# Mixed attention in a four-layer model: a mask moved from TensorE to VectorE, and a projection stage laid out anew

## The reference

```python
# first model, layers 0 and 3: three groups of 16 heads of 64; windows 128, 512, 2048, dilations 1, 4, 16
s = einsum("bnqhd,bnkhd->bnhqk", qb, kk) * scale
s = where(valid, s, NEG_INF)                 # window, dilation and causal mask
p = exp(s - logsumexp(s)); o = p @ vv        # groups are then weighed by their logsumexp
# second model
qa, ka, va, qb, ckv, iq, ik, iw = split(rmsnorm(h) @ w_in)
o_a = diff_attention(qa, ka, va)             # 4 heads: softmax 1 minus lambda times softmax 2
c = rmsnorm(ckv); q_lat = rmsnorm(einsum("blhd,hdc->blhc", qb, w_uk))
score = einsum("bqh,bqhk->bqk", iw, relu(iq . ik))   # 8 index heads
sel = top_k(score, 64)                       # keys that each query may see
o_b = softmax over sel of (q_lat . c + bias), times c, times w_uv
h = h + concat(o_a, o_b) @ w_out
```

## Time and profile before

| | |
|---|---|
| time, median of 3 runs | 2188.54 us (2186.72 to 2189.94) |
| profiled execution: its time, its span | 2189.12 us, 2187.3 us |
| TensorE busy in it | 98% of the span |
| VectorE busy, ScalarE busy | 68%, 46% |
| chain that ended last | 91% TensorE, 4% VectorE, 3% ScalarE |
| mean granted TensorE clock | 0.993 of full speed |

### The profile page before, as it was taken

How to read it: one execution, slowest core, us unless ns; L and a number is a source line. 1 busy time by engine, 2 the same in 40 slices (tenths; PEclk the granted TensorE clock), 3 DMA queues, 4 the chain that set the end, 5 groups by cost and what they waited for, 6 DMA issues and landing times.

```text
span 2187.3 us, 43087 instructions
## 1 busy us (share of the span) xinstructions
PE 2142.3 (98%) x16131; PEld 1962.9 (90%) x16131; DVE 1497.1 (68%) x2462; ACT 1005.9 (46%) x1348; POOL 483.7 (22%) x518
## 2 busy tenths in 40 slices
PE   7999999999999999999999999999999999999999
PEld 7998779988999988799889987799889998779998
DVE  6884778856688667588678847788565545566653
ACT  4334555544355553455443345555453334354342
POOL 2320004520124305034212200045213300201320
PEclk8999999999999999999999999999999999999999
DMA  5555225564645554245655552155545555305554
GB/s 177 192 179 186 77 84 182 183 204 168 206 151 191 194 181 145 68 154 191 207 165 177 191 180 90 68 179 186 203 155 172 168 178 182 104 13 162 184 185 142
DMA packets 299904, 350.28 MB, mean 160 GB/s; under 512 B 7588, under 2 KB 254950, under 8 KB 299814
## 3 DMA queue, kind: packets, MB, share of 16 engines
q1 hardware_dynamic: 298070, 347.05, 48.6%
q10 hardware_dynamic: 1360, 1.77, 0.2%
q0 software_dynamic: 384, 0.24, 0.0%
HBM read 346.35 MB, written 2.68 MB: 160 GB/s over the span
## 4 chain that ended last, share of the span: by engine, by line
PE 91%; DVE 4%; ACT 3%; DMA 2%; issue 1%; ACTq 0%; SPq 0%; DVEq 0%
PE ps L2260 26%; PE ps L2262 26%; PE ps L2261 26%; PE ps L2661 2%; PE ps L2632 1%; PE ps L2608 1%; PE ps L2619 1%; ACT w_hi L1200 1%; DVE w_lo L1634 1%; PE ps L2376 1%; PE ps L2371 1%; PE ps L2372 1%; PE ps L2308 1%; PE ps L2602 1%; DMA raw<-in_w_in_dram 0%
## 5 line engine op out<-in xcount | busy, mean ns | idle before, releaser
L1634 DVE TENSOR_TENSOR w_lo<-raw,w_hi 128x2048 fp32r<-128x2048 f32 (+3 forms) x311 | 697.1, 2241 | 456.9 <-ACT w_hi L1200 456.6
L2260 PE MATMUL ps<-a_hi,w_hi 128*128 128x256 f32 (+1 forms) x3176 | 899.4, 283 | 5.1 <-DVE w_lo L1634 4.7
L2262 PE MATMUL ps<-a_hi,w_lo 128*128 128x256 f32 (+1 forms) x3176 | 897.2, 282 | 0.0
L2261 PE MATMUL ps<-a_lo,w_hi 128*128 128x256 f32 (+1 forms) x3176 | 897.0, 282 | 0.0
L1200 ACT CAST w_hi<-raw 128x2048 fp32r<-128x2048 f32 (+3 forms) x319 | 589.9, 1849 | 557.0 <-PE ps L2262 531.7
L2260 PEld LDWEIGHTS ps<-a_hi,w_hi 128*128 128x128 f32 x3176 | 601.1, 189 | 11.5 <-DVE w_lo L1634 5.5
L2262 PEld LDWEIGHTS ps<-a_hi,w_lo 128*128 128x128 f32 x3176 | 602.0, 190 | 0.0
L2261 PEld LDWEIGHTS ps<-a_lo,w_hi 128*128 128x128 f32 x3176 | 598.8, 189 | 0.1
L2164 POOL TENSOR_TENSOR hs<-sg,cv 128x256 f32<-128x256 f32 x88 | 65.4, 743 | 672.3 <-DVE cv L2000 672.3
L2171 POOL CAST hid_hi<-hs 128x256 f32 (+3 forms) x132 | 135.9, 1029 | 300.5 <-DVE hs L2046 286.2
L2260 PE MATMUL ps<-w_hi,hid_hi 128*128 128x512 f32 x480 | 188.6, 393 | 0.8 <-DVE w_lo L1634 0.5
(11 more groups left out here) (346 smaller groups left out, 2661.7 us busy)
## 6 DMA issues: line engine op xcount, KB each, us to landing
raw<-in_ffn_w_in_dram SPq DMA_DIRECT2D x88, 1024.0 KB, 5.1
raw<-in_attn_w_qkv_dram SPq DMA_DIRECT2D x71, 1024.0 KB, 5.0
raw<-in_ffn_w_out_dram SPq DMA_DIRECT2D x32, 1024.0 KB, 5.0
raw<-in_ffn_w_gate_dram SPq DMA_DIRECT2D x22, 1024.0 KB, 5.3
raw<-in_ffn_w_up_dram SPq DMA_DIRECT2D x22, 1024.0 KB, 5.3
raw<-in_ffn_w_down_dram SPq DMA_DIRECT2D x16, 896.0 KB, 4.7
raw<-in_sc_w_in_dram SPq DMA_DIRECT2D x12, 1024.0 KB, 5.2
raw<-in_ffn_w_out_dram SPq DMA_DIRECT2D x16, 768.0 KB, 4.3
```

Of the source, the lines that this page charges most:

```text
L1634: dve.tensor_tensor(o, src, hi.bitcast(F32), ALU.subtract).then_inc(lo_ready, 1)
L2260: pe.matmul(o, wh, xh, start=start, stop=False)
L2261: pe.matmul(o, wh, xl, start=False, stop=False)
L2262: return pe.matmul(o, wl, xh, start=False, stop=stop)
```

## The change

What it does, stage by stage:

- Attention: the mask matmuls go. DVE makes one instruction of mask and maximum (`tensor_tensor_reduce`): it writes minus (score plus mask) into `prob` and the minimum of it into `nmax`; ACT then takes the exponential in place in `prob` with scale -1. `prob` has three sets instead of two. TensorE is two units of scores ahead, and a bank is free for the next scores once the maximum is taken. For odd n, ACT copies both halves of the turned probabilities. The output projection waits for seven heads before its second half of tokens.
- The four table DMAs leave SP's queue and stand on ACT's: bias and causal mask in `ckv`, `uk` and `uv` in `heads` at m = 1. The 72 columns of the index key come in by a DMA of ACT in `z` (`raw_ik`), are split on their own (`ik_hi`, `ik_low`) and are the first tile of `ckv`. The latent is two slabs of 128 columns. `latent_sum` moves behind tile 0 of `heads`. `rcol` is gone from `ckv`.
- `va` is gone as a phase: `heads` has a fourth group (m = 12 to 15) of four tiles with 272 tokens as columns, which DVE drains into `work`; TensorE turns them head by head (`turn_values`, three transposes each) and ACT copies them into `va` (`copy_values`). The `select` steps stand at m = 9 (step 0), 13 (1), 14 (2 to 6), 15 (7, 8), and in `mix2` behind units 0 to 4 (9 to 17).
- `mix2`: the copy of unit 10 goes to DVE; ACT's root behind unit 9 stands behind a copy of results; the turns of the first four heads start one unit later, behind the unit's own turn; `add` waits for the first four heads one by one.
- A few named semaphores become the general `link`.

The core of the diff:

```diff
-    z_cols = [0, 512, 1536]
+    z_cols = [0, 512, 1536, 1024]
-    phases.append(Phase("ckv", 1, K8, lambda i, j: win[:, :, 2048:2304] if j == 0 else win[:, :, 2816:2888]))
-    phases.append(Phase("heads", 3, K8, lambda i, j: win[:, :, z_cols[i] + j * SW:z_cols[i] + (j + 1) * SW]))
-    phases.append(Phase("va", 1, K8, lambda i, j: win[:, :, 1024 + j * SW:1024 + (j + 1) * SW]))
+    phases.append(Phase("ckv", 1, K8, lambda i, j: win[:, :, 2048 + j * P:2048 + (j + 1) * P]))
+    phases.append(Phase("heads", 4, K8, lambda i, j: win[:, :, z_cols[i] + j * SW:z_cols[i] + (j + 1) * SW]))
...
+        def turn_values(pe, head, B):
+            bank = 6 + head % 2
+            if head < 2:
+                pe.wait_ge(drained_a, B["da"] + 7 + head)
+                pe.wait_ge(rq_root, 1)
+                pe.wait_ge(vl_copied, 3)
+            else:
+                pe.wait_ge(drained_b, B["db"] + 7 + head - 2)
+                pe.wait_ge(va_copied, head - 1)
+            for k, (k0, kn) in enumerate(KT):
+                mm = pe.transpose(ps[0:kn, bank, k * P:(k + 1) * P], work[:, head, k0:k0 + kn], ident[:])
+            mm.then_inc(va_turned, 1)
...
+        TURN_BY_DVE = 10
+        SELECT_IN = {9: (0,), 13: (1,), 14: (2, 3, 4, 5, 6), 15: (7, 8)}
...
             for n in range(16):
                 if n + 1 < 16:
                     mix_max(dve, n + 1)
+                if n == TURN_BY_DVE + 1:
+                    turned_copy(dve, n - 1).then_inc(t2_copied, 1)
                 weigh(n)
-                if n < 4:
-                    for step in range(11 + 2 * n, min(13 + 2 * n, SEL_STEPS)):
+                if n < 5:
+                    for step in range(9 + 2 * n, min(11 + 2 * n, SEL_STEPS)):
                         select(dve, step)
...
-                if ph.kind == "ckv":
-                    sp.wait_ge(skew_stored[0], 16)
-                    sp.wait_ge(skew_stored[1], 16)
-                    sp.wait_ge(tile_done, ph.prior.base["t"])
-                    skew = bass.AP(scratch.tensor, P - 1, [[N_BIAS * SKEW - 1, P], [SKEW, N_BIAS], [1, TW]])
-                    sp.dma_start(rel2, skew).then_inc(bias_landed, 16)
-                    sp.dma_start(tmp2[:, 0, :], A["const"][:, C_CAUSAL:C_CAUSAL + TW]).then_inc(bias_landed, 16)
-                    sp.dma_start(uk[:], A["b_w_uk_2"][0].rearrange("h d c -> d h c")).then_inc(u_landed, 16)
-                    sp.dma_start(uv[:], A["b_w_uv_2"][0].rearrange("h (c p) d -> p (h c) d", p=P)).then_inc(u_landed, 16)
...
+                elif ph.kind == "z":
+                    act.wait_ge(tile_done, B["t"])
+                    act.dma_start(raw_ik[:], win[:, :, 2816:2888]).then_inc(ik_landed, 16)
...
+                    act.wait_ge(ik_landed, 16)
+                    act.copy(ik_hi[:], raw_ik[:]).then_inc(ik_cast, 1)
...
-                        at = 2 * (n % 2) + x
+                        at = 2 * (n % 3) + x
                         act.wait_ge(max_ready, u0 + 2 * n + x + 1)
-                        if n >= 2:
-                            act.wait_ge(prob_turned, u0 + 2 * (n - 2) + x + 1)
-                        act.activation(prob[:, at, :], ps[:, at, :], ACT.Exp, bias=nmax[:, at:at + 1],
+                        act.activation(prob[:, at, :], prob[:, at, :], ACT.Exp, scale=-1.0, bias=nmax[:, at:at + 1],
                                        accum_out=rsum[:, at:at + 1]).then_inc(exp_ready, 1)
...
+                        if n % 2:
+                            act.wait_ge(prob_turned, u0 + 2 * n + 2)
+                            act.copy(probT[:, 1, :], ps[:, 5, :]).then_inc(probT_ready[1], 1)
...
+                        if m == 14:
+                            split_ahead(ph, m // 4, True)
+                        if m == 15:
+                            mix_max(dve, 0)
+                        if m in SELECT_IN:
+                            for step in SELECT_IN[m]:
+                                select(dve, step)
+                    drain(15)
...
                     def row_max(n, x):
-                        at = 2 * (n % 2) + x
+                        at = 2 * (n % 3) + x
                         dve.wait_ge(scores_done, u0 + 2 * n + x + 1)
-                        dve.tensor_reduce(nmax[:, at:at + 1], ps[:, at, :], AX, ALU.max, negate=True).then_inc(max_ready, 1)
+                        if n >= 3:
+                            dve.wait_ge(prob_turned, u0 + 2 * (n - 3) + x + 1)
+                        dve.tensor_tensor_reduce(prob[:, at, :], ps[:, 2 * (n % 2) + x, :],
+                                                 maskb[:, (n % 2) * 512:(n % 2 + 1) * 512], -1.0, 3.0e38, ALU.add, ALU.min,
+                                                 nmax[:, at:at + 1]).then_inc(max_ready, 1)
...
                     for n in range(HEADS):
+                        if n + 2 < HEADS:
+                            for x in range(2):
+                                row_max(n + 2, x)
                         if n + 1 < HEADS:
                             for x in range(2):
-                                row_max(n + 1, x)
-                            for x in range(2):
                                 normalise(n + 1, x)
-                        dve.wait_ge(prob_turned, u0 + 2 * n + 2)
-                        dve.tensor_copy(probT[:, 1, :], ps[:, 5, :]).then_inc(probT_ready[1], 1)
+                        if n % 2 == 0:
+                            dve.wait_ge(prob_turned, u0 + 2 * n + 2)
+                            dve.tensor_copy(probT[:, 1, :], ps[:, 5, :]).then_inc(probT_ready[1], 1)
...
                 elif ph.kind == "ckv":
-                    pe.wait_ge(rpre_ready, ph.norm.base["chn"] + 1)
-                    for t, (t0, tn) in enumerate(KT):
-                        mm = pe.transpose(ps[0:tn, 6, 32 * t:32 * t + 32], rpre[0:32, t0:t0 + tn], ident[0:32, 0:32])
-                    mm.then_inc(rcol_done, 1)
...
+                    pe.wait_ge(ik_lo, 1)
+                    bank_free(ph, 0, 2)
+                    for k in range(KD):
+                        mm = mm3(ps[0:72, 2, 0:TW], ik_hi[:, k, :], ik_low[:, k, :], a_hi[:, k, :], a_lo[:, k, :], k == 0,
+                                 k == KD - 1)
+                    mm.then_inc(tile_done, 1)
...
                         if n >= 2:
-                            pe.wait_ge(exp_ready, u0 + 2 * (n - 1))
-                        for x in range(2):
-                            pe.matmul(ps[:, 2 * par + x, :], identb[:], maskb[:, par * 512:(par + 1) * 512], start=True,
-                                      stop=False, skip_group_check=True)
+                            pe.wait_ge(max_ready, u0 + 2 * (n - 1))
...
                     for n in range(HEADS):
-                        if n + 1 < HEADS:
-                            scores(n + 1)
+                        if n + 2 < HEADS:
+                            scores(n + 2)
```

276 lines of the change are left out of this document (132 added, 144 removed).

## The result

| | before | after |
|---|---|---|
| median, ten runs of each | 2188.42 us (2185.24 to 2192.28) | 2176.95 us (2169.89 to 2183.32) |
| ratio, 95% interval | | 0.9946, 0.9935 to 0.9958 |
| profiled execution: time, span | 2189.12, 2187.3 | 2182.15, 2180.3 |
| mean granted clock of it | 0.993 | 0.991 |
| chain that ended last | 91% TensorE | 88% TensorE, 5% VectorE, 4% ScalarE |

The kernel is faster by 11.5 us in the median (0.5%, and the interval of the ratio lies clear of 1), and the prediction of 2178.5 us holds. But the runs of the changed kernel spread over 13 us where those of before spread over 7. Sorted by their mean clock, six at 0.993 or more have a median of 2175.2 us, and four at 0.990 or 0.991 lie at 2179.7 to 2183.3. The profiled one is of the second kind, so its span shows only 7.0 us of gain.

What follows compares the result with a forecast made beforehand. TensorE, with 91% of the chain, was taken as the bound, VectorE nearly as full in the attention. Terms of 6 + 3 + 1.8 + 0.3 = 11 us gave 2177.5 from the median, stated as 2178.5; range 2169 to 2189.

Steps and rivals of the forecast that it cites:

- 6, 3, 1.8 and 0.3 us: Forecast gains: both attentions, up to the first tile of `heads`, from there to unit 5 of `mix2`, and behind it.
- The new instruction: Attention: VectorE's combined mask and maximum takes 0.76 us with its second part, bounds 0.60 and 0.94.
- Rival (a): Attention: the new instruction costs over 0.95 us and VectorE becomes the bound, up to 2203 us; chance 0.12 for slower.
- The unit: Attention: VectorE's 3.26 us against TensorE's 3.2 sets the unit, 3.3 us with waits, a gain of 0.4.
- rival (c): New instruction as cheap as a plain maximum, clock stays at 2.4 GHz in the hole: 2168 to 2172 us; chance 0.13.
- Opening and end: Attention phase: opening 1.8 us longer, some 0.3 of it given back; the last two units lose their gain, 0.8 us.
- The hole: TensorE's idle time between `z` and the index tile: over 2 us left, ending about 1828 instead of 1829.8.
- The wait ahead of `heads`: TensorE's wait for the low part of the first slab of `heads`: stays at 1.2 us.
- I let the clock fall as before: Behind the hole after `z`: the clock falls again, adding 2.1 us for the slow part.
- From `heads` to unit 5: Stretch to unit 5 of `mix2`: last tile 4.9 us earlier, 3.1 later behind it, net gain 1.8 (-2 to 4).
- Behind unit 5 the work of each engine is the same: `mix2` behind unit 5: unchanged work; relaxed waits of `add` and the earlier results' copy give 0.3 us.

## Why the prediction was right, step by step

**The time** of 2178.5 us against 2176.95 was right in part by luck, since errors on both sides cancel. I had forecast 6, 3, 1.8 and 0.3 us; the profiled executions show 10.7, 4.4, 0.9 and -7.4, and -2.7 in a place that the prediction didn't look at, with 1.2 of a chance start.

**The new instruction** was the term that decided. I took 0.76 us; it is 0.61, the lower bound. The Trainium skill, VectorE: DVE Perf Modes, in its section on two Vector instructions with no wait between them, says that an accumulator output makes two instructions: this trace agrees, with a second part of 83 ns, and it costs nothing since the next instruction starts with it. Rival (a) falls with it.

**The unit** came out as forecast, 3.29 us against 3.3, for the wrong reason. Not VectorE's sum sets it (it is idle for 0.3 us a unit). The order on ScalarE does for a good part, as the two runs with another order show: 57.2 and 56.5 us a phase with the same work. The 3.74 us from which I took the gain was the longer of two units in turn, so a unit gained 0.36 us and not 0.4, and TensorE's own work is 3.12 us and not 3.2. At 0.60 an instruction I let TensorE decide, 10 us for both phases: that bound, which is rival (c)'s, is near the 10.7 measured, though no run has all its units at 3.12. Rival (c) has the clock in the hole right too, for this execution; its 2168 to 2172 was reached by one run of ten.

**Opening and end** of the phase were mis-sized. I charged 1.5 us for four combined instructions ahead of the first normalising; from the first scores to the first values it takes 8.06 us, and took 8.15 from the first mask. The last two units, which I let lose 0.8, gained 0.6: 5.9 us from the third-last values to the last, 6.5 before. These two steps are 3 us a phase; the units between gave 4.7 us instead of 5.5. Together the attention was 2.4 us a phase too small.

**The hole.** 2.12 us idle was forecast as over 2, released by VectorE, with the index key as what is late: 4.5 us to land by forecast, 5.0 measured. The wait ahead of `heads`, which I left at 1.2, is 1.80 us, for VectorE's drains of the latent behind that low part. "I let the clock fall as before" was wrong for this execution and right for others: of the twelve traces with the new `ckv` six have the low clock there and `heads` 14.8 to 15.1 us behind `z`, six keep it, 13.4 to 13.9. Those with the fall start `heads` 2.8 to 3.0 us earlier, as I forecast. My reading of the cause, a slab held up by the tables ahead of it, is borne out by the run with the tables on SyncE: 7.7 us to land instead of 3.8, and `rpre` 3.3 us later. Its price in the hole is only 0.5 us, since the slab is halved and the index key nearly as late. The Trainium skill's rule (Trainium Kernel Development and Optimization, Key Constraints), that another issuing engine saves only the issue time, is not tested by that run: the tables change their queue and their time of issue together.

**From `heads` to unit 5** I took 4.9 us less to the last tile and 3.1 more behind it. It is 5.1 less where the clock stays (81.2 to 76.1 us) and 3.6 in the profiled run (low from 1904 to 1907), and 2.7 more behind. What is late is a whole unit, though, and not the selection, which I gave the most of the 3.1.

**"Behind unit 5 the work of each engine is the same"** is the step that failed. The work is the same, but not what the clock did: with the new order 24 of 55 runs have a mean clock of 0.991 or less, and four of the seven profiled ones were at the 1.2 GHz level for some 20 us in the tail of `mix2`. Such a fall costs 6.5 us (49.7 against 43.3 from the last tile to `add`), more than all terms that I had forecast behind the attention together. And that nothing happens in a phase that the diff doesn't touch was assumed and not argued: 2.7 us.

## What to carry to other kernels

An in-order engine's place for a short copy can set a loop in which no engine is full: look at who waits for whom in one period before summing busy times, and try the orders. Price changes in sparse stretches with the granted clock in view, and from several executions: compare runs at like clocks, since one profile can show a fall that half of the executions don't have. Where two engines hold each other up, see which one starts first: 0.2 us decides whether the low part is longer. And check the phases behind the changed one as well.

## What was not expected of the hardware

- In the sparse tail of `mix2` the clock fell to the 1.2 GHz level for about 20 us in some executions and not at all in others of the same instructions, 6.5 us of difference; the same wait of 1.63 us, and the same 3.37 us of work in 5 us around it, stand in an execution where it fell right after and in one where it stayed.
- A low part on VectorE and a small instruction on GpSimd hold each other up. In the block behind the second attention (1400 to 1530 us) 82 low parts took 2.37 us or more, in eleven traces, all with the new attention. Each of them had started 0.02 to 0.17 us behind the start of a cast on GpSimd, which takes 0.40 us; the 16 that started 0.24 to 0.38 us behind one took 2.29 or 2.30. A GpSimd instruction that starts just inside a low part takes 2.4 to 2.6 us instead of 0.40 or 0.75. In the three traces with the old attention no low part there started inside such a cast.
- Why the new attention shifts the two against each other by these tenths wasn't tried and stays open, and so does why the cast to `w_hi` is later there. It is not how early the attention ends: with one unit ahead it ended only 4.5 us earlier than before instead of 11.8, with the same loss. A slab at the block's start lands 6.2 to 6.6 us after its issue in those eleven traces, instead of 5.0 to 5.2.
